# A three-branch recurrent mixer on one core: norms and gate sums computed during the projection, level differences as TensorE products, score blocks placed over two PSUM banks

## The reference, cut to what matters

```python
def _token_mixer(h, ...):
    proj = h @ w_in       # gdn q,k,v,z,a,b | gla q,k,v,g,r | ssd z,x,B,C,dt | 3 merge gates
    # gated DeltaNet, 4 heads of 128
    q, k, v = split(silu(causal_conv(gdn_qkv)))
    q = l2norm(q) * 128 ** -0.5;  k = l2norm(k)
    g = -exp(A_log) * softplus(a + dt_bias);  beta = sigmoid(b)
    # per chunk: G = cumsum(g); dec = exp(G_i - G_j)
    #   solve (I + tril(beta * (k k^T) * dec, -1)) X = rhs; u = ... - (...) @ S
    #   o = (q * exp(G)) @ S + ((q k^T) * dec) @ u;  S = exp(G_last) * S + (k * exp(G_last - G))^T @ u
    # GLA, 4 heads of 64: a gate per token AND channel
    #   att_ij = sum_d q_id k_jd exp(Bc_id - Bc_jd),  Bc = cumsum(gk)
    # SSD, 8 heads: cumsum of a = -exp(A_log) * dt, one decay per head
    merged = sum_b sigmoid(gate_b) * (o_b @ w_br_b);  return merged @ w_out
```

## Time and profile before

| | us |
|---|---|
| median of 3 runs (lowest, highest) | 3427.71 (3424.24, 3428.06) |
| the profiled run's own time | 3428.86 |
| its span in the trace | 3427.1 |
| PE busy | 3229.5 (94%) |
| DVE busy | 1315.3 (38%) |
| ACT busy | 778.4 (23%) |
| POOL busy | 1572.4 (46%) |

### The profile page before, as it was taken

One profiled execution on the slowest core, in us unless ns is written; L12 is line 12 of the kernel. 1 busy time (PEld: TensorE's weight loads), 2 busy tenths in 40 slices (PEclk: granted clock), 3 DMA queues, 4 the chain that ended last, 5 costly groups with the idle time before them and its releaser, 6 DMA issues. The chain is left out here.

```text
span 3427.1 us, 67666 instructions
## 1 busy us (share of the span) xinstructions
PE 3229.5 (94%) x26954; PEld 3108.2 (91%) x26954; DVE 1315.3 (38%) x2171; ACT 778.4 (23%) x1447; POOL 1572.4 (46%) x948
## 2 busy tenths in 40 slices
PE   7999989988889999999999999999888899899997
PEld 7999989977669998999999999899676799899997
DVE  3331065558752214331043310753676522233301
ACT  2111032234441112111021111332434311221100
POOL 4665546610016654655545654566000266545553
PEclk9999999998979999999999999999988899999999
DMA  3222222200042222222222222222001322212221
GB/s 124 88 86 85 69 77 86 92 1 1 29 145 87 87 88 68 86 86 85 76 78 88 90 80 69 82 87 73 1 2 70 118 87 90 89 62 86 89 82 65
DMA packets 77997, 259.88 MB, mean 76 GB/s; under 512 B 8576, under 2 KB 10624, under 8 KB 77056
## 3 DMA queue, kind: packets, MB, share of 16 engines
q1 hardware_dynamic: 77536, 256.90, 23.4%
q10 hardware_dynamic: 288, 0.49, 0.1%
HBM read 242.78 MB, written 14.58 MB: 75 GB/s over the span
## 5 line engine op out<-in xcount | busy, mean ns | idle before, releaser
L510 POOL TENSOR_SCALAR wh<-raw 128x1024 fp32r<-128x1024 f32 (+1 forms) x464 | 471.8, 1017 | 1757.3 <-PE ps L551 1161.6
L512 POOL TENSOR_TENSOR wl<-raw,wh 128x1024 fp32r<-128x1024 f32 (+1 forms) x464 | 1066.8, 2299 | 67.8 <-POOL wh L510 0.3
L547 PE MATMUL ps<-hh,wh 128*128 128x272 f32 x4768 | 999.4, 291 | 67.2 <-DVE hl L1767 44.5
L549 PE MATMUL ps<-hl,wh 128*128 128x272 f32 x4768 | 994.0, 289 | 0.0
L551 PE MATMUL ps<-hh,wl 128*128 128x272 f32 x4768 | 989.5, 289 | 0.0
L547 PEld LDWEIGHTS ps<-hh,wh 128*128 128x128 f32 x4768 | 755.9, 190 | 74.9 <-issue 59.3
L549 PEld LDWEIGHTS ps<-hl,wh 128*128 128x128 f32 x4768 | 753.3, 189 | 0.0
L551 PEld LDWEIGHTS ps<-hh,wl 128*128 128x128 f32 x4768 | 752.7, 189 | 0.0
L1776 DVE SCALAR_TENSOR_TENSOR f<-f,prm,rstd_post 128x544 f32<-128x544 f32 x48 | 43.7, 916 | 653.7 <-ACT rstd_post L1276 653.7
L547 PE MATMUL ps<-ah,wh 128*128 128x272 f32 x1408 | 294.5, 291 | 0.0
L549 PE MATMUL ps<-al,wh 128*128 128x272 f32 x1408 | 290.2, 287 | 0.0
(11 more groups left out here) (421 smaller groups left out, 3678.5 us busy)
## 6 DMA issues: line engine op xcount, KB each, us to landing
raw<-in_up SPq DMA_DIRECT2D x176, 512.0 KB, 3.5
raw<-in_win SPq DMA_DIRECT2D x80, 512.0 KB, 3.5
raw<-in_merge SPq DMA_DIRECT2D x96, 384.0 KB, 3.1
raw<-in_down SPq DMA_DIRECT2D x64, 512.0 KB, 3.5
raw<-in_down SPq DMA_DIRECT2D x32, 384.0 KB, 3.2
raw<-in_wout SPq DMA_DIRECT2D x16, 512.0 KB, 3.5
states<-in_in_gdn SPq DMA_DIRECT2D x2, 2048.0 KB, 8.1
proj<-in_in_ssd SPq DMA_DIRECT2D x2, 2048.0 KB, 12.4
```

Of the source, the lines that this page charges most:

```text
L510: pool.tensor_scalar(hi, src, 1.0, 1.0, MULT, MULT).then_inc(hi_done, 1)
L512: pool.tensor_tensor(lo, src, hi.bitcast(F32), SUB).then_inc(lo_done, 1)
L547: pe.matmul(out, high, mh_[:, c], start=a, stop=False)
L549: pe.matmul(out, high, ml_[:, c], start=False, stop=False)
```

## The change

1. `common` is gone. Its work for all 544 columns is done in the projection. Behind each of windows 12 to 19 PE makes two ones-products of 128x272 for one tile of keys or queries (`key_sums`), ACT squares two tiles ahead, then takes Ln and Exp, and DVE normalizes the tile in place. Five transposes of the gate columns stand behind window 32, two running sums of 512 columns behind window 34, six small ones behind window 36. The loop of 40 windows is partly written out; some windows have an added wait.
2. In GLA's prompt chunks the level differences are PE products with a constant of zeros and ones (`dif`, 128x896, loaded once a layer): 8 products for levels 0 to 3, 6 for levels 4 to 6, into banks 4 and 5; ACT takes one Exp of each part out of PSUM. DVE's subtractions, ACT's copy of the sums and its Abs go. The sample step keeps the old way.
3. A level's scores in both banks are placed by one instruction of 512 columns; level 0 by a multiplication with its mask, so that the zeroing goes.
4. DeltaNet's first products wait for `g_oc` and `g_s` themselves; keys and queries are read in place; the three order strings are new (264 letters before, 250 or 254 now).

```diff
+            def key_sums(layer, t):
+                slot = (t + 2) % 4
+                pe.wait_ge(key_["sq"], layer * KEYS + t + 1)
+                pe.wait_ge(evict_done, layer * 40 + 12 + t + 3)
+                for h in range(2):
+                    last = pe.matmul(ps[:, 2 * slot + h, 0:HALF], ones, key_squares(t)[:, h * HALF:(h + 1) * HALF], start=True, stop=True)
+                last.then_inc(key_["ss"], 1)
...
-                with pe.Fori(0, 10) as i:
+                with pe.Fori(0, 3) as i:
                     for j in range(4):
-                        pe.wait_ge(evict_done, value(pe, layer * 40 + i * 4 + (j + 1)))
-                        product(layer, B_PROJ + 4, i, j, 4, j, KD, h_tiles)
+                        window(i, j)
+                for t in range(KEYS + 2):
+                    if t >= 2:
+                        pe.wait_ge(key_["ln"], layer * KEYS + t - 1)
+                    window(3 + t // 4, t % 4)
+                    if t < KEYS:
+                        key_sums(layer, t)
...
+                window(8, 0)
+                token_rows(layer)
+                window(8, 1)
+                pe.wait_ge(gate_["tm"], layer + 1)
+                window(8, 2)
+                running_sums(layer)
+                window(8, 3)
+                pe.wait_ge(gate_["gc"], layer + 1)
+                window(9, 0)
+                sum_rows(layer)
...
                 with act.Fori(0, 3) as i:
                     conv_group(i, 0, GQ, 0)
-                with act.Fori(0, 2) as i:
-                    direct_group(i, 3, LQ, ACT.Copy)
+                act.preload_act_table_set(LN_EXP)
+                act.wait_ge(csil_done, layer * CONV_TILES + KEYS + 2)
...
+                for t in range(2):
+                    square(t)
+                for t in range(KEYS):
+                    block_in(0, 3, t)
+                    act.activation(halves(proj[:, LQ + t, :]), pair(t % 4), ACT.Copy).then_inc(evict_done, 1)
+                    act.wait_ge(key_["ss"], layer * KEYS + t + 1)
+                    act.activation(halves(key_squares(t)), pair((t + 2) % 4), ACT.Ln, bias=epsc).then_inc(key_["ln"], 1)
+                    act.wait_ge(key_["ln"], layer * KEYS + t + 1)
+                    act.activation(key_squares(t), key_squares(t), ACT.Exp, scale=-0.5).then_inc(key_["rs"], 1)
+                    if t + 2 < KEYS:
+                        square(t + 2)
                 narrow_columns(layer)
...
                 with dve.Fori(0, 3) as i:
                     conv_group(i, 0, 0)
+                for t in range(KEYS):
+                    dve.wait_ge(key_["rs"], layer * KEYS + t + 1)
+                    dve.scalar_tensor_tensor(out=proj[:, GQ + t, :], in0=proj[:, GQ + t, :], scalar=GDN_SCALE if t < 4 else 1.0,
+                                             in1=key_squares(t), op0=MULT, op1=MULT).then_inc(key_["n"], 1)
                 narrow_columns(layer)
...
-                pe.wait_ge(g_["brb"], value(pe, o + 1))
-                pe.wait_ge(both["rg"], further(pe, o + 1))
+                pe.wait_ge(g_["oc"], o + 1)
+                pe.wait_ge(g_["s"], o + 1)
...
-                level_magnitudes(step, L)
-                yield
-                level_decays(step, L)
-                yield
+                yield
+                for part in range(2):
+                    act.wait_ge(l_["dl"], difference(step, part))
+                    a, m = PARTS[part][0], len(PARTS[part])
+                    act.activation(L["dl"][:, a:a + m, :].rearrange("p l t -> p (l t)"),
+                                   ps[:, 4:6, :].rearrange("p b c -> p (b c)")[:, 0:m * 256], ACT.Exp).then_inc(l_["d2"], 1)
...
-                for e in range(2):
-                    last = dve.copy_predicated(view(L["att"][0:n, e * w:(e + 1) * w], 2), over(cst[0:n, c:c + n], 2).bitcast(U32),
-                                               view(ps[0:n, 4 + e, 0:w], 2))
+                if l == 0:
+                    last = dve.tensor_tensor(att_, mask, found, MULT)
+                else:
+                    last = dve.copy_predicated(att_, mask.bitcast(U32), found)
 TENSOR_ORDER = (
-    "clcglslcgglgsgllgglsgslsgnlglglglgnlnnnglgnglnnngnnclcgslgllglsglgnglnslsggsglgslgglnngclglglgsl"
+    "shlgslgnlssglsglgnglgnhlglglglglgnlglglgnlgnnhhnlglgngslnlnghnslggnlglglglhsglgsslglslglglglngll"
```

## The result

Median of 16 runs 3431.41 us (3427.36 to 3437.23) against 3425.33 us (3419.21 to 3429.53) for the kernel before on the same chips; ratio 1.0018, 95% interval 1.0011 to 1.0025. The change makes the kernel slower by 6 us, less than the 6.9 us which the prediction took as the least that could be told from no change. Forecast were 3431 us and a difference of 1.8 us. The median before was 2.4 us lower here than in the first three runs, so the difference is larger than that of the sum, though the time itself was met.

What follows compares the result with a forecast made beforehand. PE bounds the projection, a chain going between engines the mixer. Projection loses 27.9 us, mixer gains 27.0: 0.9 a layer, 1.8 in both, on 3428.86, giving 3431 us; range 3400 to 3458.

Steps and rivals of the forecast that it cites:

- PE's wait behind window 12: Projection: PE idles at the first key sums until ACT's square is ready; 14.2 us, from 12 to 19.
- c0, c1, c2, c3: Mixer prompt chunks: first chunk's head 1.5 us shorter, then 54.4, 51.1, 51.5 us between state updates against 56.9, 57.0, 58.7.
- sample step: Mixer's last step: SSD's part starts about 6 us sooner, head products go; gain 10 of 66 us, from 6 to 12.
- the relief by POOL: Projection: idle PE stops POOL, so DVE's copies and taps run faster and the wait shortens by 5.0 us.
- third rival: Projection: POOL's stop does not speed DVE, so the wait is 19 us; 3441 us in all, chance 0.03.
- What is left of this path is ... 3.7: Mixer chunk head, state update to decays: update, eight spreads and one Exp remain, 3.7 us.
- its second part: Mixer sign: 54, 51 and 52 us between state updates; wrong if chunks take 57 again or fall under 50.
- 14 x 0.24 = 3.4 a chunk: Mixer: level-difference products ahead of the solve's first products on PE give back part of 3.4 us a chunk, some hidden.
- second rival: Mixer: the solve takes up what the head gives, mixer gains 15 us a layer; 3455 us, chance 0.23.
- Placing: GLA scores on DVE: 32 instructions at 0.70 us replace 64 of 440 ns, saving 5.8 us over four chunks.
- the first forecast: Whole kernel: projection loss and mixer gain are of one size; 3431 us, own range 3420 to 3444, chance 0.43.
- first rival: Mixer gives more, 34 or up to 38 us a layer; 3409 us in all, chance 0.31.

Runs made afterwards that it cites:

- e1: Changed kernel with key sums paired, two tiles at a time behind windows 16 to 19 instead of one behind each of 12 to 19; 3399.04 us, ratio 0.9922.
- e7: Changed kernel without 10 of the 14 level-difference products a chunk, for timing only; 3431.46 us, ratio 1.0020.
- e5: Changed kernel with level differences back on DVE, ACT taking Abs and Exp together in the place of its first Exp; 3457.65 us, ratio 1.0099.
- e2: Kernel before with only the new placing: one instruction over both banks, level 0 by mask product, no zeroing; 3422.45 us, ratio 0.9986.
- e6: The e1 kernel with the second scaling of GLA's states moved behind the `u_bb` copy in ACT's sample-step list; 3409.5 us, ratio 0.9952.
- e9: Kernel before with 14 dummy 128x128 products in each prompt chunk, placed ahead of the solve's first products; 3443.12 us, ratio 1.0042.
- e3: Changed kernel with the old placing, two instructions a level and zeroing; 3434.97 us, ratio 1.0021.

## Why the prediction was right, and where not

The time and the direction of both terms were right: a loss in the projection and a gain of about its size in the mixer. That the time was met so closely (3431.41 for 3431) is in part luck. The projection cost 2.9 us a layer less than forecast, the mixer gave 4.3 less on the mean of the two layers, and the sum started from a run of 3428.86, 3.5 us above the median that the kernel before showed later. Step by step, us for one layer:

| step | forecast | measured |
|---|---|---|
| PE's wait behind window 12 | 14.2 | 13.5 and 13.9 |
| key sums | 7.4 | 6.3 for seven, 1.6 for the first at half clock |
| gate products | 4.1 | 4.0 (windows 0.5, 1.8 and 1.8 later than 6.0) |
| half clock after the wait | 1.7 | 1.9 (window 13 took 7.85) |
| other waits | 0.5 | none in PE; windows of the written list take 6.00, not 6.05, about -1.3 |
| projection | 27.9 | 25.4 and 24.6 |
| prompt chunks | -17 | -16.9 and -25.0 (the memset before them comes 1.7 us later behind the table load) |
| of these c0, c1, c2, c3 | -1.5, -2.5, -5.9, -7.2 | -5.8, -0.7, -0.4, -10.0 and -6.8, -3.9, -4.4, -9.9 |
| sample step | -10 | -3.1 and -3.9 |
| mixer, from table load to merge | -27 | -18.3 and -27.1 |

**The wait.** Every part of its working is in the trace: the lag of the convolutions, the table load, the square, and the relief by POOL. The relief was 5.9 us, not 5.0 (the last silu ends at 558.03, and at 563.97 in the kernel before). Without it the wait would have been 13.5 + 5.9 = 19.4 us, the 19 of the third rival. The lesson in e1 is that the same lag could be had for nothing: window 16 ends 24 us after window 12, and ACT is ready by 569.6.

**The head.** "What is left of this path is ... 3.7" was 4.0. But the chunks' total came out near the forecast in layer 0 by errors of opposite sign, and that is luck. By the prediction's own signs its second part was off: it named chunks of 54, 51 and 52 us and called itself wrong if they fell under 50, and chunk 3 took 48.8 in both layers, while chunks 1 and 2 of layer 0 stayed at 56.2 and 56.6. One error is the step "14 x 0.24 = 3.4 a chunk" that "goes back": e7, with ten of the 14 products gone, shows 0.8 us in chunk 1, 1.3 in chunk 2 and nothing in chunks 0 and 3. Another is that I gave the differences' removal from DVE and ACT no own value beyond DVE's busy time; e5 shows up to 26 us, with its order and its low clock mixed in. The second rival's reason (the solve takes up what the head gives) was not tested by itself. What held the gain down in layer 0 against layer 1 is the clock in chunks 1 and 2: 56.2 at 0.94 against 53.0 at 1.00 for the same instructions.

**The clock.** The prediction had no term for it in the mixer, and it goes through the whole gain. At equal clock the chunks differ far less than the table's lengths: chunk 2 took 57.1 us at 0.91 before and 55.6 at 0.91 in e1, and 55.5 at 0.94 in e2 against 54.2 at 0.94 in e6. The changed kernel's chunk 3 stood at 1.00 where the old one stood at 0.91, and was 10 us shorter. So a good part of what the mixer gave came together with a higher clock. Whether shorter waits raised it is not shown; in e9, where products filled PE's waits, it rose by 0.01 to 0.03 only.

**Placing.** Forecast 0.70 us a level, measured 0.73. The saving was put too high all the same: the prediction took 64 x 0.440 = 28.2 us for the old way, where the group's busy time is 24.7 because neighbours overlap, so 1.6 us are saved and not 5.8, and 1.9 by the zeroing. That placing does not bound the prompt chunks is shown by e3. A small slip beside it: six small products at 0.24 are 1.4, not 1.2, in the sum of the gate products; they and the transposes measured less.

**The sample step** is the term that was mis-sized: 10 forecast, 3 to 4 measured. Its head did shorten, from 11.5 to 4.0 us between the last update and the decays (952.49 - 948.45). But SSD's part was to begin 6 us sooner. It begins 16.1 us behind the state's update in layer 0 and 15.2 in layer 1 (2661.64 - 2646.47), where it was 17.4, and still waits for a norm of chunk 3 (`ol`). In layer 1 GLA's scalings (line 1543, twice 2.43 us) now stand among SSD's steps:

```profile
2661.64 0.42 ACT L1607 ACTIVATE u_xbc<-proj 128x256 f32<-128x256 f32 x1 [0.84 <-DVE ol L2396]
...
2664.10 2.43 ACT L1543 ACTIVATE proj<-proj,t_eb 128x128 f32<-128x128 f32 x8
...
2669.61 0.57 ACT L1619 ACTIVATE u_bb<-ps 128x512 f32<-128x512 f32 x1
```

In the kernel before they stood behind, and the same two steps were as far apart:

```profile
2655.42 0.42 ACT L1551 ACTIVATE u_xbc<-proj 128x256 f32<-128x256 f32 x1 [0.40 <-DVE ol L2313]
...
2663.44 0.60 ACT L1563 ACTIVATE u_bb<-ps 128x512 f32<-128x512 f32 x1 [2.42 <-PE ps L1127]
```

It is 8.0 us in both, since before ACT waited there for PE. So the scalings did not lengthen this part, and e6, which moved one of them away, made the time worse. What missed is the start of SSD's part, 1 to 2 us sooner and not 6; why the norm did not come sooner no run shows.

**The whole.** With 18.3 us from the mixer in layer 0 and 27.1 in layer 1, against 25.4 and 24.6 for the projections, the balance is that of the first forecast, a loss and a gain of one size, and no rival came in. The first rival (34 to 38 us from the mixer) was not reached by any kernel; the sum of the mixer's shortest values in the changed and the paired kernel (48.6, 53.0, 52.7, 48.8, 63.5) is 28 us below before. In e1 the mixers come near it (27.6 and 25.2 below) and the projection costs 9.9 us (720.88 against 711.01), and the whole came to 3399.

## What to carry to other kernels

Before a product is put behind a given window of a loop in which PE never waits, look up in the timeline when the other engine is really through: a lag that costs nothing while four buffers take it up becomes a wait of its full length for the engine that is the bound. Then move the product to where the lag has been worked off, two at a time if buffers are few; here that was worth 32 us (3431.4 to 3399.0). And price moved work by where it stands in the in-order lists: the same instructions in three orders differed by 30 us, while ten products more or less on PE made no difference in the median. Before a row is blamed for a delay, look up when its input was ready: twice here (the copy in e5, `u_bb` in e6) the row in front was not what held it up. And read a stage's length only with its granted clock beside it.

## What the runs showed of the hardware that was not expected

- The granted clock of one and the same stretch varies from execution to execution: chunk 1 was seen at 53.0, 54.6 and 56.2 us with 1.00, 0.97 and 0.94, chunk 2 at 52.7, 54.1, 55.6 and 56.6 with 0.97, 0.94, 0.91 and 0.88, while chunk 3 took 48.7 or 48.8 us in every layer of the changed and the paired kernel. The sample step of the paired kernel was seen at 63.5, 64.8 and 67.7 us with 0.72, 0.68 and 0.62. In the kernel before chunks 1 to 3 stood at 0.91 in its trace.
- Dummy products raised the clock of the prompt chunks only from 0.91 to 0.92 to 0.94, for 14 of them in each chunk, and cost 15 us. Four of 512 columns in each of two long waits brought the merge's start from 0.50 to 1.00 (6.4 us in place of 8.7 for the same pairs), but took 6.5 and 4.8 us themselves, and the time did not change by an amount that can be told.
- Two fp32 products of 272 columns between windows cost 0.90 us, as in the FFN (0.92); the five transposes of 128 columns cost 0.5 us together, less than half of what I had taken from the products (1.2).
